# First MLP input product: one 512-column matmul per high weight tile in place of two of 256

## What is computed

```python
h2 = modulate(rms_norm(x, g_pre_mlp[l]), sh2, sc2)
ff = jnp.square(jax.nn.relu(h2 @ w_mlp_in[l])) @ w_mlp_out[l]
x = x + gt2[:, None, :] * rms_norm(ff, g_post_mlp[l])
```

## Time and profile before

| | us |
|---|---|
| runs | 843.07, 845.57, 845.21 (median 845.21) |
| profiled execution, its own time | 842.66 |
| its span, first to last instruction | 840.9 |
| mean granted TensorE clock | 0.943 |
| busy PE / weight loads / DVE / ACT / POOL | 780.0 / 740.0 / 532.6 / 380.6 / 145.4 |

### The profile page before, as it was taken

How to read it: one execution, slowest core, us unless ns; L and a number is a source line. 1 busy time by engine, 2 the same in 40 slices (tenths; PEclk the granted TensorE clock), 3 DMA queues, 4 the chain that set the end, 5 groups by cost and what they waited for, 6 DMA issues and landing times. The chain is left out here.

```text
span 840.9 us, 13944 instructions
## 1 busy us (share of the span) xinstructions
PE 780.0 (93%) x5979; PEld 740.0 (88%) x5979; DVE 532.6 (63%) x688; ACT 380.6 (45%) x524; POOL 145.4 (17%) x141
## 2 busy tenths in 40 slices
PE   3599999998959999999978989899799999999997
PEld 3599989998949999999976988687589999999997
DVE  5887667687484766644345868967755575655441
ACT  3444333444632555534423534577644544444441
POOL 1500110002020000000013499604000122221000
PEclk9599999999959999999997968999799999999998
DMA  9979566669533765565631541141605376555511
GB/s 353 356 261 317 176 201 199 190 212 308 193 101 108 242 221 195 190 203 195 198 111 50 155 146 51 50 152 50 200 1 178 124 251 195 173 171 188 189 38 51
DMA packets 125937, 145.99 MB, mean 174 GB/s; under 512 B 4052, under 2 KB 118964, under 8 KB 125876
## 3 DMA queue, kind: packets, MB, share of 16 engines
q1 hardware_dynamic: 124512, 143.32, 52.1%
q10 hardware_dynamic: 1364, 1.79, 0.6%
HBM read 144.05 MB, written 1.05 MB: 173 GB/s over the span
## 5 line engine op out<-in xcount | busy, mean ns | idle before, releaser
L1368 DVE TENSOR_TENSOR w_lo<-raw,w_hi 128x2048 fp32r<-128x2048 f32 (+2 forms) x112 | 245.9, 2198 | 155.3 <-ACT w_hi L979 155.1
L979 ACT ACTIVATE w_hi<-raw 128x2048 fp32r<-128x2048 f32 (+2 forms) x114 | 207.4, 1824 | 254.6 <-PE bank L566 237.1
L566 PE MATMUL bank<-act_hi,w_hi 128*128 128x256 f32 x816 | 236.9, 290 | 4.5 <-ACT act_hi L1096 3.6
L566 PE MATMUL bank<-act_hi,w_lo 128*128 128x256 f32 x816 | 234.0, 287 | 2.7 <-DVE w_lo L1368 2.7
L566 PE MATMUL bank<-act_lo,w_hi 128*128 128x256 f32 x816 | 234.5, 287 | 0.0
L566 PEld LDWEIGHTS bank<-act_hi,w_hi 128*128 128x128 f32 x816 | 159.9, 196 | 8.0 <-issue 7.9
L566 PEld LDWEIGHTS bank<-act_hi,w_lo 128*128 128x128 f32 x816 | 159.9, 196 | 3.1 <-DVE w_lo L1368 3.1
L566 PEld LDWEIGHTS bank<-act_lo,w_hi 128*128 128x128 f32 x816 | 160.0, 196 | 0.7 <-DVE act_lo L1585 0.3
L566 PE MATMUL bank<-hidden_hi,w_hi 128*128 128x256 f32 x432 | 121.2, 281 | 0.0
L566 PE MATMUL bank<-hidden_hi,w_lo 128*128 128x256 f32 x432 | 121.0, 280 | 0.0
L566 PE MATMUL bank<-hidden_lo,w_hi 128*128 128x256 f32 x432 | 121.0, 280 | 0.0
(11 more groups left out here) (263 smaller groups left out, 1059.1 us busy)
## 6 DMA issues: line engine op xcount, KB each, us to landing
raw<-in_w_in SPq DMA_DIRECT2D x31, 1024.0 KB, 5.8
raw<-in_w_ada SPq DMA_DIRECT2D x24, 1024.0 KB, 6.4
raw<-in_w_gate_up SPq DMA_DIRECT2D x22, 1024.0 KB, 5.2
raw<-in_w_mlp_in SPq DMA_DIRECT2D x16, 1024.0 KB, 6.4
raw<-in_w_mlp_out SPq DMA_DIRECT2D x16, 1024.0 KB, 4.9
raw<-in_w_out SPq DMA_DIRECT2D x8, 1024.0 KB, 8.7
raw<-in_w_down SPq DMA_DIRECT2D x8, 1024.0 KB, 5.1
raw<-in_w_down SPq DMA_DIRECT2D x4, 768.0 KB, 4.7
```

The costliest lines, as they stand in the source:

```text
L566: i = e.matmul(dst, lhs, rhs, start=start and k == 0 and m == 0 and n == 0, stop=stop and k == kt - 1 and n == 2, skip_group_check=True)
L979: e.activation(w_hi[slot][:, 0:kt * n_cols], raw[i % N_RAW][:, 0:kt * n_cols], ACT.Copy).then_inc(hi_split, 1)
L1368: e.tensor_tensor(w_lo[slot][:, 0:kt * n_cols], raw[i % N_RAW][:, 0:kt * n_cols], w_hi[slot][:, 0:kt * n_cols].bitcast(F32), ALU.subtract) ...
```

## The change

1. Each pair of tiles becomes one: `act_both` is 128 x 8 x 2 x 256, with `hi` and `lo` of a channel tile beside each other; `act_hi` and `act_lo` are views of it. The same is done for `mixed`, `heads`, `hidden`, `ffn` and `hidden2`. All products read through such a tile.
2. In the first MLP input alone `passes` gives way to `halves`: for each k and m one matmul of 512 columns with `w_hi` (high and low activations side by side) into a bank of its own for each m, and one of 256 columns with `w_lo` into that bank's left half. 32 matmuls a product in place of 48, two banks in place of one. PE waits for both `hi` and `lo` of a tile before its first matmul.
3. ACT copies the right half (the low part) of each of the two banks to the buffer, in place of one relu of 512 columns. DVE adds the left half to it, twice 256 columns, and relu and square become one instruction of 512 columns, which waits for both adds. A bank is free when DVE's add of it is done.
4. Four semaphores (`scale1_set`, `gain1_set`, `scale2_set`, `gain2_set`) become one counter `gains_set`, in the same order on DVE; nothing else moves.

```diff
+        def alloc_pair(stack, name, tiles):
+            both = alloc(stack, name, [P, tiles, 2, T], F32R)
+            return both, both[:, :, 0, :], both[:, :, 1, :]
...
-        act_hi = alloc(fixed, "act_hi", [P, DT, T], F32R)
-        act_lo = alloc(fixed, "act_lo", [P, DT, T], F32R)
+        act_both, act_hi, act_lo = alloc_pair(fixed, "act_both", DT)
...
-            hidden_hi = alloc(own, "hidden_hi", [P, FT, T], F32R)
-            hidden_lo = alloc(own, "hidden_lo", [P, FT, T], F32R)
+            hidden_both, hidden_hi, hidden_lo = alloc_pair(own, "hidden_both", FT)
...
         for i in range(FT // 2):
-            banks.use(MLP1 + i, relu_set, i + 1)
+            for m in range(2):
+                banks.use((MLP1 + i, m), hid_summed, 2 * i + m + 1)
...
+            def halves(p, o, both, ready, k):
+                slot = p % N_SPLIT
+                kt, n_cols = tiles_of(p)
+                wh = w_hi[slot][:].rearrange("p (k c) -> p k c", k=kt)
+                wl = w_lo[slot][:].rearrange("p (k c) -> p k c", k=kt)
+                for m in range(n_cols // P):
+                    cut = slice(m * P, (m + 1) * P)
+                    if m == 0:
+                        pe.wait_ge(hi_split, p + 1)
+                        pe.wait_ge(*ready[k][0])
+                        pe.wait_ge(*ready[k][1])
+                    e.matmul(o[m][:], wh[:, k, cut], both[:, k, :, :].rearrange("p a t -> p (a t)"), start=k == 0,
+                             stop=False, skip_group_check=True)
+                    if m == 0:
+                        pe.wait_ge(*low_ready(p))
+                    i = e.matmul(o[m][:, 0:T], wl[:, k, cut], both[:, k, 0, :], start=False, stop=k == kt - 1,
+                                 skip_group_check=True)
+                if k == kt - 1:
+                    i.then_inc(product_done, 1)
...
-            two_products(MLP1, start_bank(MLP1), start_bank(MLP1 + 1), act_hi, act_lo, ready_h2)
+            first_banks = [[start_bank((p, m)) for m in range(2)] for p in (MLP1, MLP1 + 1)]
+            for k in range(DT):
+                for j in range(2):
+                    halves(MLP1 + j, first_banks[j], act_both, ready_h2, k)
             for p in range(MLP1 + 2, MLP2):
-                product(p, start_bank(p), act_hi, act_lo, ready_h2)
+                o = [start_bank((p, m)) for m in range(2)]
+                for k in range(DT):
+                    halves(p, o, act_both, ready_h2, k)
                 if p == GATE2_SUM_AFTER:
                     modulation_sum(GATE2)
...
(ACT, loop over i)
-                e.activation(relu[i % 4], pair(bank[banks.bank[p]]), ACT.Relu).then_inc(relu_set, 1)
+                for m in range(2):
+                    e.activation(relu[i % 4][:, m, :], bank[banks.bank[p, m]][:, T:2 * T], ACT.Copy).then_inc(low_half, 1)
                 act.wait_ge(relu_squared, i + 1)
...
(DVE, loop over i)
-                dve.wait_ge(relu_set, i + 1)
-                e.tensor_tensor(r, r, r, ALU.mult).then_inc(relu_squared, 1)
+                for m in range(2):
+                    b = bank[banks.bank[p, m]]
+                    dve.wait_ge(low_half, 2 * i + m + 1)
+                    e.tensor_tensor(r[:, m, :], b[:, 0:T], r[:, m, :], ALU.add).then_inc(hid_summed, 1)
+                dve.wait_ge(hid_summed, 2 * i + 2)
+                e.scalar_tensor_tensor(out=r, in0=r, scalar=0.0, in1=r, op0=ALU.max, op1=ALU.mult).then_inc(relu_squared, 1)
                 dve.wait_ge(hid_hi, i + 1)
```

More of the change, by code:

```diff
@@ L541, in start_bank, with passes @@
                 return bank[banks.bank[key]]
-            def passes(p, o, hi, lo, ready, k, k0, start, stop, tokens_first=False):
+            def passes(p, o, both, ready, k, k0, start, stop, tokens_first=False):
                 slot = p % N_SPLIT
@@ L550, in passes @@
                 for m in range(n_m):
[L551 removed]
+                    for n, (wp, ap) in enumerate(((wh, 0), (wh, 1), (wl, 0))):
                         if m == 0:
@@ L569, in passes, with product, two_products @@
                     i.then_inc(product_done, 1)
-            def product(p, o, hi, lo, ready, k0=0, start=True, stop=True, tokens_first=False):
+            def halves(p, o, both, ready, k):
[17 more added lines that the diff above has]
+                    i.then_inc(product_done, 1)
+            def product(p, o, both, ready, k0=0, start=True, stop=True, tokens_first=False):
                 for k in range(tiles_of(p)[0]):
-                    passes(p, o, hi, lo, ready, k, k0, start, stop, tokens_first)
-            def two_products(p, o, o1, hi, lo, ready):
+                    passes(p, o, both, ready, k, k0, start, stop, tokens_first)
+            def two_products(p, o, o1, both, ready):
                 for k in range(DT):
-                    passes(p, o, hi, lo, ready, k, 0, True, True)
-                    passes(p + 1, o1, hi, lo, ready, k, 0, True, True)
+                    passes(p, o, both, ready, k, 0, True, True)
+                    passes(p + 1, o1, both, ready, k, 0, True, True)
             def transpose_rows(group):
@@ L661, in tensor_program @@
                     stick_output(step - 2)
-                product(p, start_bank(p), act_hi, act_lo, ready_h1, tokens_first=(name == "v"))
+                product(p, start_bank(p), act_both, ready_h1, tokens_first=(name == "v"))
                 if p == 2 * ADA_CHUNKS - 1:
@@ L698, in tensor_program @@
                 for r in range(PARTS):
-                    product(MLP2 + i * PARTS + r, o, hidden_hi, hidden_lo, ready_hid, k0=r * CHUNK_TILES,
+                    product(MLP2 + i * PARTS + r, o, hidden_both, ready_hid, k0=r * CHUNK_TILES,
                             start=(r == 0), stop=(r == PARTS - 1))
@@ L907, in tensor_program @@
             for i in range(DT // 2):
-                product(OUT2 + i, start_bank(OUT2 + i), act_hi, act_lo, ready_mix2)
+                product(OUT2 + i, start_bank(OUT2 + i), act_both, ready_mix2)
                 if i >= 2:
@@ L1005, in scalar_program @@
             root(0, D, 1)
-            act.wait_ge(scale1_set, 2)
+            act.wait_ge(gains_set, 2)
             act.wait_ge(x_copied, DT // 2)
@@ L1076, in scalar_program @@
             high_after(product_at[OUT1 + 1])
-            act.wait_ge(gain1_set, 1)
+            act.wait_ge(gains_set, 3)
             act.wait_ge(merged_lo, DT // 2)
@@ L1118, in scalar_program @@
                 if i == 0:
-                    act.wait_ge(gain2_set, 1)
+                    act.wait_ge(gains_set, 6)
                     act.wait_ge(h2_lo, DT)
@@ L1575, in vector_program @@
             dve.wait_ge(rstd_set, 3)
-            dve.wait_ge(scale2_set, 2)
+            dve.wait_ge(gains_set, 5)
             dve.wait_ge(res_dve, RES_DVE)
```

58 lines of the change are left out of this document (27 added, 31 removed).

## The result

The changed kernel took 846.92 us (median of 17 runs, 843.61 to 851.0) where the kernel before took 842.61 in the same session (839.98 to 847.29): a ratio of 1.0051, 95% interval 1.0035 to 1.0068. It is slower, as forecast, but by 4.3 us and not by 8.3; and the forecast of 853.5 stood on a median of three runs, 845.21, where 17 runs now give the kernel before 842.61. Run again beside other kernels it gave 1.0077 (1.0059 to 1.0096), 6.7 us. The profiled execution took 846.58 with a span of 844.6, against 842.66 and 840.9. Ratios leave out single runs over 1.5% above the fastest of the same kernel (1099.86 us was one of the kernel before).

The account below looks back on a forecast made before the run. PE was taken as the bound, by 0.36 us an iteration over a closed ACT-DVE loop. Lateness of 7.7 + 0.6 = +8.3 us on the 845.21 median gave 853.5, range 847.5 to 859.

Parts of the forecast that it names:

- The loop: First MLP input: the closed chain of ACT and DVE steps goes from 5.40 to 6.25 us an iteration, +0.85.
- the square has two inputs and a scalar ... +0.06: DVE's fused relu-and-square, first MLP input: 0.49 us for 256 columns where the plain form takes 0.42, so +0.06.
- the sum: Whole kernel: weights 7.7 us late at the third MLP output product, 0.6 more at the next, total +8.3 us.
- 8.8 with a `w_ada` chunk: First MLP input: ACT's `w_hi` starts lie 8.8 us apart in iterations with such a chunk, 6.25 otherwise.
- PE's part: First MLP input: a 512- and 256-column pair takes 0.347 us against 0.360; 3.3 us saved if PE alone set the pace.
- The estimate of 0.325: First MLP input: a matmul pair by the skill page's issue gaps, 0.216 and 0.109 us; the saving would be 8.7 us.
- The new wait: Before the fourth first-MLP-input product: PE idles 3.6 us for a bank until DVE's first adds; not a sum to add.
- rival C: First MLP input: the 3.6 us idle drops PE's clock, costing 2.7 us or twice that, 856 to 859; chance 0.06.
- The start: First matmul of the first MLP input: PE also waits for `act_lo`, losing one column slot, 0.2 us.
- rival D: Interleaved tiles change matmul steps elsewhere: +6.1 us (859.6) if slower, -4.9 us (848.6) if faster; chance 0.05.
- every later stage 8.3 later: After the first MLP input: nothing more lost or won back, so all later stages start 8.3 us later.

Follow-up runs that it names:

- adds_only: Kernel before with the interleaved tiles and merged semaphore, old matmuls, and two extra 256-column DVE operations before the square: ratio 1.0117; repeated, 1.0125.
- reorder_early: Changed kernel with `hidden_hi` and `hidden_lo` made one iteration late and DVE's adds and square of the first iteration done earlier: ratio 0.9936 to the kernel before.
- no_adds: Changed kernel without DVE's adds; ACT takes relu of the high half and the low half is left out of the result: ratio 0.9942 to the kernel before.
- first_adds_early: Changed kernel with DVE's adds and square of the first iteration done between the two low parts ahead of them: ratio 1.0062 to the kernel before.
- wait_both: Kernel before, with PE also waiting for `act_lo` ahead of the first MLP's first matmul: ratio 1.0008.
- the second profile: Profile of the changed kernel's later runs, code not altered again; run again beside other kernels it gave ratio 1.0077 to the kernel before.

## Why the prediction was right or wrong

- **The loop** was right in mechanism. +0.85 an iteration was forecast, +0.78 came: "the square has two inputs and a scalar ... +0.06" was wrong (0.69 us with and without the scalar, at 512 columns), and first add to square was 0.78 as forecast from the earlier trace rows (0.34 + 0.45). The stage gave +7.34 where the sum had 8.1 after the start. adds_only shows that this is all the loop's. One sign was wrong: "8.8 with a `w_ada` chunk" takes 2.5 us for each chunk, but such an iteration took 6.71 before (5.40 + 1.31) and 7.50 after (6.18 + 1.32). The sum didn't use that figure.
- **PE's part**: a pair takes 0.353 (5.65 us for 16 in reorder_early), near the 0.347 forecast. The estimate of 0.325 worked out with the Trainium skill's page (TensorE: Matmul & The Clock Gate, Back-to-back issue gap) is not reached. The saving was 1.9 (reorder_early) to 2.5 us (no_adds) in the stage, with 3.3 forecast.
- **The new wait**: 3.25 for 3.6, at the place forecast, an instalment of the loop's cost (first_adds_early: 0.7 in the stage).
- **The clock** (rival C): the idle time was followed by 3.1 us at half clock, and the loop swallowed it; nothing came on top.
- **The start**: 0.2 for the wait on `act_lo` is neither shown nor refuted (0.15 in wait_both, inside the spread). The profiled run was 2.65 us earlier at D1 (0.6 in the second profile). 0.8 of it is the phase of the clock in the first pair of products, and 1.4 was gained by the high copy that starts at 108.27 before and at 106.86 after, all of it in the stretch from 89 to 100 us, whose code is the old one; its granted clock was 0.85 before and 1.00 after. None of this is the edit's. In the profiles of kernels with the old places of tiles D1 lies anywhere from 258.4 to 263.6.
- **The layout** (rival D) changed no step: right.
- **The base**: the 853.5 is 6.6 us above the 846.92 measured. 2.6 of it is the median of three runs of the kernel before, 845.21, against 842.61 over 17; the other 4.0 is the difference, 8.3 forecast and 4.3 measured. With the better base the same sum would have said 850.9.
- **The step that failed** is the sentence "and every later stage 8.3 later". I counted the two banks of a product inside MLP1 only, and took every later wait as unchanged. But the ring's position runs on through the plan: behind the edit each product has another bank, and the head stages lose a wait of 2.65 us and win 3.4 + 2.3 us in two intervals, of which 1.1 to 4.0 goes again in the five after them. The lost wait is shown to be the banks'; the rest goes with the granted clock there, which two kernels with the old banks had as well. The sum for the profiled run is then +7.34 in the stage, -2.65 at the start, +0.19 between, -1.18 over all head stages: +3.7, the difference of the spans. In the second profile +7.39, -0.64, +0.33 and -4.12: +2.9, again the difference of the spans. So in the first profile the larger part of what is missing from 8.3 is the start, which isn't the edit's, and in the second it is the heads.
- **Still open**: the runs put the changed kernel 4.3 and 6.7 us above the one before, its profiles 3.7 and 2.9; the adds-only kernels are 10 us above in the runs and 8.2 and 7.4 in the profiles. That leaves 0.6 to 3.8 us not placed. The granted clock varies from run to run by as much: the 17 runs of before in the last session lie between a mean clock of 0.951 (840.18 us) and 0.939 (845.41), and between 839.78 and 847.3 us. Nor is the worth of the bank phase from end to end settled: nil in the kernel before, 3 to 4 us with the adds.

## What to carry to other kernels

Before work moves from the busiest engine to a second one, follow the chain of handovers between the others: a loop of two engines with 0.36 us of slack an iteration turned a saving on PE into a loss, at 65% busy DVE. Open the loop (use a result one iteration late) together with such a move: the late order alone was worth nothing, the edit alone was a loss, both with the first adds early were 0.6% faster, of which 1.9 us (0.2%) in the stage itself. And when an edit changes how many slots a round-robin plan hands out, compare every later slot's holder too: here one free bank took away a wait of 2.65 us in a stage far behind the edit, though its worth over the whole kernel isn't settled, and the same shift undone cost 13 us in another stage.

## What the hardware showed that I had not expected

The step of a 256-column matmul was 0.120, 0.118, 0.116 or 0.113 us depending on where the activation tile lay against the weights, which on this kernel is worth 2.2%; and on the same tiles it went from 0.113 to 0.118 and back where PE's stream was broken by 0.55 us of idle time or by sixteen matmuls of one column. An instruction with a scalar and two tensor inputs took the same 0.69 us for 512 columns as the plain product of two tensors. And one and the same interval of 33 to 35 us, with the same instructions, ran at a mean granted clock of 0.95 in one profile of the changed kernel and of 0.86 in the other.
